# Experts' tokens of pairs 1 to 7 fetched as rows by an indirect DMA and turned on TensorE

## What is computed

```python
def grouped_moe(x, router_w, router_bias, w_gate, w_up, w_down):
    ...
    gates = jnp.sum(jax.nn.one_hot(e_idx, N_EXPERTS, dtype=jnp.float32) * w[..., None], axis=1)

    def step(acc, ew):
        g_e, wg_e, wu_e, wd_e = ew
        h = jax.nn.silu(x2 @ wg_e) * (x2 @ wu_e)
        return acc + (h @ wd_e) * g_e[:, None].astype(x2.dtype), None

    out, _ = lax.scan(step, jnp.zeros_like(x2), (gates.T, w_gate, w_up, w_down))
```

## Time and profile before

| | us |
|---|---|
| median of 3 runs (lowest 1517.3, highest 1529.44) | 1520.92 |
| the profiled execution's own time | 1519.31 |
| its span, first to last instruction | 1517.6 |
| experts, first layer: first product of pair 0 to last addition into the sum | about 209 to 443 |
| experts, second layer | about 663 to 897 |

### The profile page before, as it was taken

How to read it: one execution, slowest core, us unless ns; L and a number is a source line. 1 busy time by engine, 2 the same in 40 slices (tenths; PEclk the granted TensorE clock), 3 DMA queues, 4 the chain that set the end, 5 groups by cost and what they waited for, 6 DMA issues and landing times.

```text
span 1517.6 us, 14938 instructions
## 1 busy us (share of the span) xinstructions
PE 1365.9 (90%) x6082; PEld 870.9 (57%) x6082; DVE 441.8 (29%) x961; ACT 279.4 (18%) x602; POOL 61.1 (4%) x97
## 2 busy tenths in 40 slices
PE   7868869999979996879999969998899996999997
PEld 6755434444435774444444438875676685888743
DVE  0993231211130233231111140355502304222201
ACT  4032121001010333030011022141234303000000
POOL 4910000000000000000000000000000000000000
PEclk9978879999999995889999989999999998999998
DMA  9510459999993050459999990331131033444420
GB/s 359 192 78 1 166 195 417 423 427 427 423 360 125 1 187 35 160 215 418 423 427 427 421 334 28 111 111 56 56 111 56 0 111 111 160 132 152 166 83 28
DMA packets 78614, 307.94 MB, mean 203 GB/s; under 512 B 5826, under 2 KB 30142, under 8 KB 64719
## 3 DMA queue, kind: packets, MB, share of 16 engines
q1 hardware_dynamic: 72064, 298.85, 50.4%
q10 hardware_dynamic: 6479, 8.07, 1.7%
HBM read 305.86 MB, written 1.06 MB: 202 GB/s over the span
## 4 chain that ended last, share of the span: by engine, by line
PE 85%; DVE 11%; issue 1%; ACT 1%; ACTq 0%; DMA 0%; DVEq 0%; POOL 0%; POOLq 0%
PE psum L234 36%; PE psum L1302 15%; PE psum L1335 7%; PE psum L565 6%; PE psum L2515 5%; PE psum L1347 3%; DVE arena L898 3%; PE psum L779 2%; PE psum L753 2%; PE psum L446 1%; PE psum L1477 1%; PE psum L1475 1%; PE psum L2173 1%; DVE x_nat L518 1%; DVE x_nat L516 1%
## 5 line engine op out<-in xcount | busy, mean ns | idle before, releaser
L234 PE MATMUL psum<-xT,ring 128*128 128x256 f32 (+2 forms) x1792 | 408.9, 390 | 6.3 <-POOLq L426 5.2
L234 PEld LDWEIGHTS psum<-xT,ring 128*128 128x128 f32 x1792 | 343.9, 193 | 67.4 <-issue 10.9
L1302 PE MATMUL psum<-ring,arena 128*64 128x512 f32 x768 | 169.6, 594 | 1.7 <-issue 1.7
L1302 PEld LDWEIGHTS psum<-ring,arena 128*64 128x64 f32 x768 | 54.8, 137 | 104.8 <-issue 104.8
L234 PE MATMUL psum<-arena 128*128 128x128 f32 (+4 forms) x684 | 91.1, 289 | 9.6 <-issue 6.3
L234 PEld LDWEIGHTS psum<-arena 128*128 128x128 f32 (+2 forms) x684 | 82.9, 195 | 13.9 <-issue 9.9
L1211 DVE TENSOR_TENSOR arena<-psum,arena 64x512 f32<-64x512 f32 x32 | 34.3, 1072 | 193.3 <-ACT arena L1259 193.3
L1335 PE MATMUL psum<-ring,arena 128*64 128x512 f32 x384 | 85.0, 595 | 0.0
L2515 PE MATMUL psum<-ring,arena 128*128 128x512 f32 x176 | 75.7, 592 | 0.0
L898 DVE SCALAR_TENSOR_TENSOR arena<-arena,vec 128x256 f32<-128x256 f32 x150 | 74.5, 572 | 0.7
L1259 ACT ACTIVATE arena<-psum 64x512 f32<-64x512 f32 x32 | 18.9, 591 | 260.3 <-PE psum L1302 260.3
(11 more groups left out here) (306 smaller groups left out, 1335.6 us busy)
## 6 DMA issues: line engine op xcount, KB each, us to landing
ring<-in_moe_w_gate SPq DMA_DIRECT2D x24, 2048.0 KB, 11.1
ring<-in_moe_w_up SPq DMA_DIRECT2D x24, 2048.0 KB, 15.7
ring<-in_moe_w_down SPq DMA_DIRECT2D x24, 2048.0 KB, 16.4
ring<-in_w_in SPq DMA_DIRECT2D x11, 2048.0 KB, 13.9
ring<-in_w_up SPq DMA_DIRECT2D x22, 1024.0 KB, 7.7
arena<-in_moe_w_gate SPq DMA_DIRECT2D x8, 2048.0 KB, 11.9
ring<-in_a_w_pw SPq DMA_DIRECT2D x6, 2048.0 KB, 17.9
ring<-in_w_down SPq DMA_DIRECT2D x5, 2048.0 KB, 7.9
```

The costliest lines, as they stand in the source:

```text
L234: last = nc.tensor.matmul(dst, lhsT, rhs, start=(n == 0), stop=(n == len(pairs) - 1))
L1302: last = pe.matmul(bank(j)[part, :], tokens[:, k, side * SEATS:side * SEATS + SEATS], weights(u + n, k), start=(k == 0), stop=(k == KC - 1))
```

## The change

Pair 0 is fetched as before. For pairs 1 to 7 the gather by multiplication is replaced:

1. In `route`, ACT stores the tokens (both halves of `by_row`, 1 MB) to a scratch tensor in HBM, `x_rows`, after it has written them. Each layer does so.
2. `turn_seats` and the copy of its result move one pair ahead: pair 0's is done before the loop, and in pair p the matrix of pair p + 1 is turned. `gatedT` has three buffers in place of two. `seat` is only called for pair 0.
3. After that copy, DVE multiplies the non-zero places of the turned matrix by a row of token numbers and sums along the row (one instruction over 128 x 256). This gives for each of the 128 seats the number of its token, or 0 for an empty seat. A second, tiny instruction makes it an integer in `token_index`.
4. POOL waits for that number and issues an indirect DMA: for each seat one row of 1024 values (4 KB) from `x_rows`, into one of two halves of the memory of `by_row`.
5. `fetch` on PE waits for that DMA and turns the rows: 8 transposes in place of 16 products.
6. Semaphores that were made per layer are shared, with waits that count on.

```diff
@@ route, ACT
                 act_step(act.activation(by_row[:, t, :, :], x_nat[:, t + 1, :].rearrange("p (f k) -> p k f", k=KC),
                                         ACT.Copy))
+            act.dma_start(x_rows.rearrange("(t p) n -> p t n", p=P), by_row[:, :, :, :].rearrange("p t k f -> p t (k f)")).then_inc(rows_stored, 16)
             act.activation(x_nat[:, 1:3, :], x_nat[:, 1:3, :], ACT.Copy, scale=ALPHA)
...
+        @block.gpsimd
+        def _(pool):
+            for p in range(1, PAIRS_E):
+                pool.wait_ge(tokens_known, LAST * layer + p)
+                if p == 1:
+                    pool.wait_ge(rows_stored, 16 * (layer + 1))
+                job_ready(pool, B + 1 if p <= 2 else job("X1", p - 3))
+                pool.indirect_dma_start(rows_in[:, p % 2, :, :].rearrange("p k f -> p (k f)"), None, x_rows,
+                                        bass.IndirectOffsetOnAxis(ap=token_index[:, p % 2:p % 2 + 1], axis=0)
+                                        ).then_inc(rows_loaded[p % 2], 16)
...
             def turned_seats(p):
-                j = job("S", p)
+                j = seat_turn(p)
                 job_ready(dve, j)
-                dve.tensor_copy(gatedT[:, p % 2, :], bank(j)[:, 0:2 * P]).then_inc(bank_free[j % BANKS], 1)
+                ins = dve.tensor_copy(gatedT[:, p % 3, :], bank(j)[:, 0:2 * P])
+                ins.then_inc(bank_free[j % BANKS], 1)
+                if p:
+                    read_out(dve, j)
+                    dve_step(dve.scalar_tensor_tensor(token_of, gatedT[:, p % 3, :], 0.0, token_row, ALU.is_gt, ALU.mult,
+                                                      accum_out=token_sum[:, p % 2:p % 2 + 1]))
+                    if p > 2:
+                        dve.wait_ge(rows_loaded[p % 2], 16 * loads(p - 2))
+                    dve.tensor_copy(token_index[:, p % 2:p % 2 + 1], token_sum[:, p % 2:p % 2 + 1]).then_inc(
+                        tokens_known, 1)
...
+            turned_seats(0)
             for p in range(PAIRS_E):
                 if p < LAST:
-                    seat(p + 1)
+                    gate_seats(p + 1)
                 hidden(0, p)
-                turned_seats(p)
+                if p < LAST:
+                    turned_seats(p + 1)
                 hidden(1, p)
                 if p < LAST:
-                    gate_seats(p + 1)
                     gathered(job("X1", p))
                 summed(p)
...
             def fetch(half, p):
 
                 j = gathers(p)[half]
-                pe.wait_ge(seats_ready, p + 1)
+                if p == 0:
+                    pe.wait_ge(seats_ready, layer + 1)
+                    free(j)
+                    gather(half, bank(j)).then_inc(job_done, 1)
+                    return
+                pe.wait_ge(rows_loaded[p % 2], 16 * loads(p))
                 free(j)
-                gather(half, bank(j)).then_inc(job_done, 1)
+                for c in range(4):
+                    last = pe.transpose(bank(j)[:, c * P:c * P + P], rows_in[:, p % 2, 4 * half + c, :], ident[:, :])
+                last.then_inc(job_done, 1)
...
             fetch(0, 0)
             fetch(1, 0)
+            turn_seats(0)
             for p in range(PAIRS_E):
                 for j in gathers(p):
                     read_out(pe, j)
                 gate_up(0, p)
-                turn_seats(p)
+                if p < LAST:
+                    turn_seats(p + 1)
                 gate_up(1, p)
```

More of the change, by code:

```diff
@@ L48 @@
 IN_PAIR = {x: n for n, x in enumerate(("GU0", "S", "GU1", "T", "X0", "X1", "Y0", "Y1"))}
-IN_LAST = {x: n for n, x in enumerate(("GU0", "S", "GU1", "T", "Y0", "Y1"))}
+IN_LAST = {x: n for n, x in enumerate(("GU0", "GU1", "T", "Y0", "Y1"))}
 PAIR_JOBS = len(IN_PAIR)
-MOE_JOBS = 2 + PAIR_JOBS * (PAIRS_E - 1) + len(IN_LAST)
+MOE_JOBS = 3 + PAIR_JOBS * (PAIRS_E - 1) + len(IN_LAST)
 BANKS = 4
@@ L256, in pair_job @@
     def pair_job(layer, p, kind):
-        return FJ[f"moe{layer}"] + 2 + PAIR_JOBS * p + (IN_LAST if p == PAIRS_E - 1 else IN_PAIR)[kind]
+        return FJ[f"moe{layer}"] + 3 + PAIR_JOBS * p + (IN_LAST if p == PAIRS_E - 1 else IN_PAIR)[kind]
     MOE_UNITS = 3 * EXPERTS
@@ L941, in program @@
     gate_col = carve(14415, 1)
-    by_row = carve(4640, 2, KC, P)
     seatsT = carve(10790, 2 * P)
     y_pair = carve(13300, D)
-    gated, gatedT = carve(15020, 2, P), carve(15280, 2, 2 * P)
+    by_row = carve(4640, 2, KC, P)
+    gated, gatedT = carve(15020, 2, P), carve(15280, 3, 2 * P)
+    token_row, token_of = carve(16048, 2 * P), carve(16304, 2 * P)
+    rows_in = by_row
+    x_rows = nc.dram_tensor("x_rows", (SEQ, D), F32).ap()
+    token_sum = small[:, 56:58]
+    rows_stored, tokens_known = sem("x_rows_stored"), sem("tokens_known")
+    rows_loaded = [sem("rows_loaded0"), sem("rows_loaded1")]
     over_w, over_y, over_hi = norm_rows[:, :, :, :].rearrange("p a b n -> p (a b n)"), y_pair, gatedT[:, 0, :].rearrange("p (r n) -> p r n", r=2)
@@ L951, in route @@
     def route(layer):
-        aff_ready, won_ready = sem(f"aff_ready{layer}"), sem(f"won_ready{layer}")
         J = FJ[f"route{layer}"]
@@ L969, in _ @@
                 dve.wait_ge(inputs_loaded, INPUT_DMAS * 16)
-            dve.wait_ge(aff_ready, 1)
+            dve.wait_ge(aff_ready, layer + 1)
             dve.tensor_tensor(sel, aff, router_b[:, :].unsqueeze(1).broadcast_to([P, 2, EXPERTS]),
@@ L999, in _ @@
                               ALU.mult).then_inc(won_ready, 1)
-            dve.wait_ge(won_ready, 1)
+            dve.wait_ge(won_ready, layer + 1)
             dve_step(dve.tensor_tensor(gates[:, :, :], beats, aff, ALU.mult))
@@ L1026, in _ @@
             take_bank(J + 1)
-            pe.wait_ge(won_ready, 1)
+            pe.wait_ge(won_ready, layer + 1)
             n = EXPERTS
@@ L1158, in _ @@
             where_over(dve, body)
+    seats_ready, gated_ready, silu_ready, scattered, cleared = (
+        sem(x) for x in ("seats_ready", "gated_ready", "silu_ready", "scattered", "sum_cleared"))
+    aff_ready, won_ready = sem("aff_ready"), sem("won_ready")
     def experts(layer):
@@ L1183, in gathers, with loads, seat_turn @@
             return (B, B + 1) if p == 0 else (job("X0", p - 1), job("X1", p - 1))
+        def loads(p):
+            return layer * ((PAIRS_E - 1) // 2 + p % 2) + (p + 1) // 2
+        def seat_turn(p):
+            return B + 2 if p == 0 else job("S", p - 1)
+        @block.gpsimd
[8 more added lines that the diff above has]
+                                        ).then_inc(rows_loaded[p % 2], 16)
         @block.vector
@@ L1208, in hidden @@
                 part = UP_IN[side]
-                dve.wait_ge(silu_ready, 2 * p + side + 1)
+                dve.wait_ge(silu_ready, 2 * (PAIRS_E * layer + p) + side + 1)
                 by_row = lambda x: x.rearrange("s (f k) -> s k f", k=DE // P)
@@ L1234, in _ @@
             dve.memset(psum[:, BANKS:2 * BANKS, :], 0.0).then_inc(cleared, 1)
+            for half in range(2):
+                dve_step(dve.tensor_scalar(token_row[:, half * P:half * P + P], counting[:, :], float(half * P - 1), None,
+                                           ALU.add))
+            turned_seats(0)
             for p in range(PAIRS_E):
                 if p < LAST:
-                    seat(p + 1)
+                    gate_seats(p + 1)
                 hidden(0, p)
-                turned_seats(p)
+                if p < LAST:
+                    turned_seats(p + 1)
                 hidden(1, p)
                 if p < LAST:
-                    gate_seats(p + 1)
                     gathered(job("X1", p))
@@ L1246, in _ @@
                 for half in range(2):
-                    dve.wait_ge(scattered, 2 * t + half + 1)
+                    dve.wait_ge(scattered, 4 * layer + 2 * t + half + 1)
                     cols = slice(half * 512, half * 512 + 512)
@@ L1306, in turn_seats @@
             def turn_seats(p):
-                j = job("S", p)
+                j = seat_turn(p)
                 free(j)
-                pe.wait_ge(gated_ready, p + 1)
+                pe.wait_ge(gated_ready, PAIRS_E * layer + p + 1)
                 for t in range(2):
@@ L1340, in scatter @@
             def scatter(p):
-                read_out(pe, job("S", p))
+                read_out(pe, seat_turn(p))
                 read_out(pe, job("Y0", p))
@@ L1346, in scatter @@
                     for half in range(2):
-                        last = pe.matmul(psum[:, BANKS + 2 * t + half, :], gatedT[:, p % 2, t * P:t * P + P],
+                        last = pe.matmul(psum[:, BANKS + 2 * t + half, :], gatedT[:, p % 3, t * P:t * P + P],
                                          y_pair[:, half * 512:half * 512 + 512], start=False, stop=(p == LAST),
@@ L1359, in _ @@
                 gate_up(0, p)
-                turn_seats(p)
+                if p < LAST:
+                    turn_seats(p + 1)
                 gate_up(1, p)
                 if p == 1:
-                    pe.wait_ge(cleared, 1)
```

(1 more changed line is left out.)

4 lines of the change are left out of this document (1 added, 3 removed).

## The result

| | median us | runs | lowest to highest |
|---|---|---|---|
| before | 1523.11 | 4 | 1517.3 to 1529.44 |
| after | 1550.32 | 4 | 1545.17 to 1552.91 |

The ratio is 1.0166, with a 95% interval of 1.014 to 1.0192. The forecast was no change, 1520.7 with a range of 1512 to 1547. The profiled execution of after took 1552.91 us, with a span of 1551.1.

The account below looks back on a forecast made before the run. Weight transfers were taken to bound the kernel, already slower than PE: room plus holes less row traffic left 0.2 us gain in the first layer and 0 in the second, so 1520.9 became 1520.7 us, range 1512 to 1547.

Parts of the forecast that it names:

- The gather on PE: In pairs 1 to 7, eight transposes take 0.88 us in place of 3.57, saving 2.69 us a pair, 37.7 for 14.
- The ceiling of the weights: At pair 7's second `gate_up`, weight transfers at 425 GB/s allow 0.2 us gain in the first layer, 0 in the second.
- row traffic is free: Rival: rows take no time from the weights in the layers, winning 19 us, 1502; chance 0.06 together with PE alone.
- The rows' delay: At PE's new wait before the transposes, rows land 1.8 to 3.2 us late a pair, ends 0.8 and 5.3.
- up to 2.69 us it only uses up what PE saved: At PE's wait for rows, lateness up to 2.69 us costs nothing extra, as the weights would have taken that saving anyway.
- rows too late: Rival: beyond 2.69 us, each microsecond of PE's wait for rows costs 14 us; 5.0 late gives 1553; much late, chance 0.24.

Follow-up runs that it names:

- e6: The change with rows only for pairs 6 and 7, asked for one pair earlier, other pairs gathering by products; ratio to before 0.9916, median 1508.28 us.
- e3: The change without its indirect DMAs and the waits for them, so experts get wrong tokens; ratio to before 0.9878, median 1506.6 us.
- e1: The change with each pair's rows asked for one pair earlier, four buffers, same traffic; ratio to before 1.0038, median 1528.82 us.
- e2: The change with three products, result overwritten, in front of PE's wait for the rows in every pair; ratio to before 1.001, median 1523.43 us.
- e4: The change without row traffic, wrong tokens, PE waiting for a chain of 27 small clears on POOL; ratio to before 0.9958.
- e5: The change without row traffic, wrong tokens, PE waiting for a chain of 32 small clears on POOL; ratio to before 1.0289.
- e7: The change with rows only for pairs 5 to 7, asked for one pair earlier, other pairs gathering by products; ratio to before 0.9965, median 1516.89 us.

## Why the forecast was wrong, by its steps

*The gather on PE*, 2.69 us a pair: right. e6's chain has 3.63, 0.44, 0.87 and 7.09 us in a row.

*The ceiling of the weights*: right. e3 gives 0.988, forecast as the rival "row traffic is free" at 1502 and measured at 1506.6. e1 puts pair 7 within 1 us of its old place in both layers; its median is 5 us from that of before.

*The rows' delay*: right in size, 1.8 to 3.2 us forecast, 2.1 to 4.3 measured, 3.0 on average. Its parts are right too: 9.1 to 10.5 us plus 1 for POOL, measured 10.5 to 11.6 with 0.94 of POOL in it. The price of the Trainium skill that was weighed there (DMA: Bandwidth & Descriptors, Anatomy of one DMA), 3.2 us as an estimate, is far from it; the page names no traffic beside the DMA. The other one (its Queues, rings and completion order), that an engine drains typically 9 to 17 descriptors before it turns to another queue, does not show in the records either: 125 rows to 111 packets of weights.

*The step that failed* is the sentence behind it: "up to 2.69 us it only uses up what PE saved". It priced a wait of PE at its own length. By length alone the waits would cost 41.6 - 37.7 = 3.9 us, about 1525. In the trace each of the 14 waits for rows costs its length and, after it, 1.86 us of slower work at the lower clock. With 3.0 + 1.86 = 4.9 us against 2.69 the loss is 2.2 us a pair, 30 us for 14. I had named the clock at the end of the forecast, said that nothing bounds it, and gave it no price and no chance. The trace of before had rows to bound it. Pair 0's gather stands behind a wait of 6.34 us; the clock there is 0.50, and its 32 products take 5.18 us, against 3.57 in pair 1.

```profile
203.20:206.00 2.80, 2.80 (x13) 2.80 (x14) 0.00 (x0) 0.00 (x0) 0.00 (x0) 0.50 0.18 59
```

*The rival "rows too late"* gave 1553 us at 5.0 us late. The measured 1550 is near it by luck: the delay was 3.0 us, and 1.9 of clock made it act as one of 4.9. Its place was right, its price per microsecond too, and its threshold was too high by the clock.

The Trainium skill describes the mechanism (TensorE: Matmul & The Clock Gate, HAM oscillation): a wait for a transfer that comes back with every tile lets the clock fall again each time, and every next tile starts cold. This trace agrees, 14 times of 14. But the page has it where the work between two waits is shorter than the wait, and has the clock stay up where the work is much longer. Here some 28 us of work stand between waits of 2.1 to 4.3 us and the clock fell all the same; the measurement decides. So the mechanism deserved a chance, and a price from the rows of before. With the 1.9 us measured even a delay of 2.1 us is over the threshold.

*Not accounted for*: the 4.6 us more behind the second layer. The kernels of the experiments have 621.8 to 625.7 us there, also those without rows, so it is not an effect of the rows. They all carry the rest of the change, and what sets this part stays open.

## What to carry to other kernels

Before making an engine's work shorter, read the room of the transfers behind it at the last piece of the loop: here 8.3 us were left in the first layer, and no saving on PE beyond that and the 1.3 us of holes could be kept. Price a new wait of TensorE as its length plus what the clock may lose behind it; where it couldn't be avoided here, work that is thrown away cost less (e2). A gather from memory must be asked for long enough ahead for its packets to take turns with the stream beside it, and used only in as many turns as the stream has room for.

## What the runs showed of the hardware

In the change, an indirect DMA of 128 rows of 4 KB kept POOL for 0.94 us and landed 10.5 to 11.6 us after its issue, beside a weight queue at 425 GB/s. Its packets of 4 KB went about one for one with packets of 8 and 16 KB (125 to 111 in 5 us).

TensorE's clock stayed at 1.00 at 12 waits of 1.4 us (e4). It fell to the lower level at all 14 waits of 2.07 to 4.3 us in the change, at two of 2.9 us in e4 and at 14 of 3.2 us and more in e5, and the eight transposes and `down` then took 1.86 us longer in all (the change, pair 7). Those waits stood between transposes. At ten waits of 2.3 to 2.8 us before products with weights (e1, e3, e7) it fell five times, so the length of the wait alone doesn't decide it.
